# Branch, merge and output projections of a hybrid decoder step as three single-pass products, with the splitting on three engines

## The reference, cut to what matters

```python
def back(x, gates, y_ssm, y_swa, y_mem, lw):
    gt = jax.nn.sigmoid(gates.astype(jnp.float32)).astype(x.dtype)
    gt = gt.reshape(gates.shape[0], gates.shape[1], N_BRANCHES, D_MODEL)
    merged = (gt[:, :, 0] * jnp.einsum('ble,ed->bld', y_ssm, lw['w_br_ssm'])
              + gt[:, :, 1] * jnp.einsum('ble,ed->bld', y_swa, lw['w_br_swa'])
              + gt[:, :, 2] * jnp.einsum('ble,ed->bld', y_mem, lw['w_br_mem']))
    x1 = x + jnp.einsum('bld,de->ble', merged, lw['w_out'])
    b, L = x1.shape[0], x1.shape[1]
    h = rms_norm(x1, lw['norm2_g']).reshape(b * L, D_MODEL)
    return x1 + hier_moe(h, lw).reshape(b, L, D_MODEL)
```

## Time and profile before

| | us |
|---|---|
| median of 3 runs | 1034.17 (1033.91 to 1037.94) |
| the profiled execution | 1034.25 |
| its span, first to last instruction | 1032.4 |
| TensorE busy | 925.0 |
| VectorE, ScalarE, GpSimd busy | 460.8, 261.7, 189.3 |

### The profile page before, as it was taken

How to read it: one execution, slowest core, us unless ns; L and a number is a source line. 1 busy time by engine, 2 the same in 40 slices (tenths; PEclk the granted TensorE clock), 3 DMA queues, 4 the chain that set the end, 5 groups by cost and what they waited for, 6 DMA issues and landing times. The chain is left out here.

```text
span 1032.4 us, 14711 instructions
## 1 busy us (share of the span) xinstructions
PE 925.0 (90%) x6134; PEld 723.4 (70%) x6134; DVE 460.8 (45%) x800; ACT 261.7 (25%) x448; POOL 189.3 (18%) x91
## 2 busy tenths in 40 slices
PE   4899968899999896887879999999996999998888
PEld 3899968799988784554657677888785655554454
DVE  3621988932277636685376941111214122222222
ACT  5347433335344453322123230000001001010100
POOL 2347754326300003022212320000000000000000
PEclk9899988979999997898889999999995799998899
DMA  6354713323522213664556979547463479999992
GB/s 248 135 203 134 275 52 117 136 83 123 169 82 83 67 62 123 243 241 164 167 204 202 377 242 398 213 175 273 145 263 123 164 325 421 422 422 422 422 422 116
DMA packets 33640, 223.41 MB, mean 216 GB/s; under 512 B 3776, under 2 KB 4048, under 8 KB 9008
## 3 DMA queue, kind: packets, MB, share of 16 engines
q1 hardware_dynamic: 28048, 199.57, 49.8%
q0 software_dynamic: 5536, 23.06, 6.8%
HBM read 207.29 MB, written 15.31 MB: 216 GB/s over the span
## 5 line engine op out<-in xcount | busy, mean ns | idle before, releaser
L469 PE MATMUL bank<-at_r,at_r 128*128 128x264 f32 (+1 forms) x1152 | 153.9, 297 | 23.4 <-POOL at_r L229 16.2
L469 PEld LDWEIGHTS bank<-at_r,at_r 128*128 128x128 f32 x1152 | 150.3, 200 | 25.6 <-POOL at_r L229 18.0
L457 PE MATMUL bank<-HN,W 128*128 128x264 f32 x640 | 157.4, 401 | 0.0
L229 POOL TENSOR_TENSOR at_r<-W,at_r 128x1024 fp32r<-128x1024 f32 x52 | 128.3, 2473 | 124.3 <-ACT at_r L1264 124.2
L457 PEld LDWEIGHTS bank<-HN,W 128*128 128x128 f32 x640 | 124.5, 198 | 30.8 <-issue 9.6
L1237 ACT ACTIVATE M<-bank 128x264 f32<-128x264 f32 (+4 forms) x140 | 59.2, 429 | 256.1 <-PE bank L469 101.5
L457 PE MATMUL bank<-M,W 128*128 128x264 f32 x384 | 87.7, 388 | 4.0 <-DMA W<-in_w_stream 1.6
L926 PE MATMUL bank<-M,W 128*128 128x128 f32 (+1 forms) x432 | 83.1, 326 | 3.3 <-DVE M L1977 3.3
L457 PEld LDWEIGHTS bank<-M,W 128*128 128x128 f32 x384 | 72.2, 190 | 17.3 <-DMA W<-in_w_stream 2.5
L926 PEld LDWEIGHTS bank<-M,W 128*128 128x128 f32 (+1 forms) x432 | 63.5, 202 | 24.6 <-issue 6.7
L1264 ACT ACTIVATE at_r<-W 128x1024 fp32r<-128x1024 f32 x60 | 62.5, 1053 | 0.6 <-DMA W<-in_w_stream 0.5
(11 more groups left out here) (318 smaller groups left out, 1086.1 us busy)
## 6 DMA issues: line engine op xcount, KB each, us to landing
W<-in_w_stream SPq DMA_DIRECT2D x70, 1024.0 KB, 4.9
M<-in_w_exp_gate SPq DMA_DIRECT2D x32, 1024.0 KB, 22.7
M<-in_w_exp_up SPq DMA_DIRECT2D x32, 1024.0 KB, 23.7
M<-in_w_exp_down SPq DMA_DIRECT2D x32, 1024.0 KB, 15.7
M<-in_state_ssm POOLq DMA_DIRECT2D x8, 1024.0 KB, 7.6
M<-in_mem_kT SPq DMA_DIRECT2D x8, 1024.0 KB, 5.9
out_s_ssm<-M POOLq DMA_DIRECT2D x8, 1024.0 KB, 11.7
M<-in_mem_v SPq DMA_DIRECT2D x8, 1024.0 KB, 7.2
```

The lines of the kernel that those rows point to most:

```text
L229: return eng.tensor_tensor(low, x, high.bitcast(F32), ALU.subtract)
L457: mm = pe.matmul(bank[:, 0:n], w[:, k, P * c:P * (c + 1)], x[:, k, 0:n], start=(k == 0), stop=(k == KT - 1))
L469: mm = pe.matmul(bank[:, 0:n], w[:, k, :], x_[:, k, 0:n], start=(k + i == 0), stop=(k == KT - 1 and i == 2))
```

## The change

Branch, merge and output products become split tiles. Each chunk gives two halves, numbered h = 0 to 39: window branch 0 to 7, memory branch 8 to 15, state-space branch 16 to 31 (each chunk pair: first part of both tiles, second part of both), output 32 to 39. ScalarE copies the high part of half h into one of three places, after half h-3 has been used; GpSimd makes the low part of even halves, VectorE of odd ones, in the place of the raw weights. The operands are split too: the attended window and memory operands after gate tile 29 on ScalarE and, after the last state store, on GpSimd; their sample columns on ScalarE and VectorE; y in two halves on ScalarE, then GpSimd and VectorE; MERGED tile by tile on ScalarE and VectorE. The window tiles all come ahead of the memory tiles. The sigmoid of the gates is taken in pieces from gate tile 29 on. The loads of the first experts' pieces go to other places, and later.

```diff
-for _i in range(4):
-    STREAM += [(("swa", _i), "w_br_swa", CW * _i, 0), (("memb", _i), "w_br_mem", CW * _i, 0)]
+for _name, _w in (("swa", "w_br_swa"), ("memb", "w_br_mem")):
+    STREAM += [((_name, _i), _w, CW * _i, 0) for _i in range(4)]
...
+        BRANCH = [("swa", i) for i in range(4)] + [("memb", i) for i in range(4)]
+        BRANCH += [(f"ssm{part}", i) for i in range(4) for part in "ab"] + [("out", i) for i in range(4)]
+        HALVES = 2 * len(BRANCH)
+        SWA_AT, MEMB_AT, SSM_AT, OUT_AT = 0, 8, 16, 32
...
 # TensorE
-            wait_drained(pe, ("mo", 3))
-            wait_drained(pe, "s_back")
-            for i in range(4):
-                for kind, x in (("swa", Q), ("memb", MQ)):
-                    w = arrive((kind, i))
-                    for c in range(2):
-                        feature_tile((kind, 2 * i + c), w, c, x, T, (kind, i))
+            def branch_half(h, bank, x, first, start, stop):
+                pe.wait_ge(sem("branch_low1" if h % 2 else "branch_low0"), h // 2 + 1)
+                high, low = branch_high(h), branch_raw(h, w_low)
+                for k in range(KT):
+                    for i, (w, part) in enumerate(((high, 0), (high, 1), (low, 0))):
+                        mm = pe.matmul(bank[:, 0:T], w[:, k, :], x(part, first + k), start=(start and k + i == 0),
+                                       stop=(stop and k == KT - 1 and i == 2))
+                return mm
...
+            pe.wait_ge(sem("sample_split"), 1)
+            pe.wait_ge(sem("attended_low"), 1)
+            for m in range(8):
+                branch_tile(("swa", m), SWA_AT + m, swa_split)
+            pe.wait_ge(sem("attended_low"), 2)
+            for m in range(8):
+                branch_tile(("memb", m), MEMB_AT + m, memb_split)
...
-            pe.wait_ge(sem("merged"), 8)
+            pe.wait_ge(sem("merged_low"), 8)
...
 # SP
-                if name == ("memb", 0):
+                if name == ("swa", 2):
+                    sp.wait_ge(sem("s_v_out"), 16)
+                    load_piece("gate", 0, 0, 0)
+                    sp.dma_start(HN, ins["xT"]).then_inc(sem("x_again"), 16)
+                elif name == ("swa", 3):
                     wait_filled(sp, "s_back")
-                    wait_filled(sp, ("mo", 3))
-                    sp.wait_ge(sem("s_v_out"), 16)
                     sp.wait_ge(sem("samples_done"), 1)
...
+                elif name in (("memb", 0), ("memb", 1)):
+                    load_piece("gate", 2 + name[1], 0, 2 + name[1])
+                elif name == ("ssmb", 0):
+                    wait_filled(sp, ("memb", 7))
                     load_piece("up", 0, 0, 0)
+                elif name == ("ssma", 1):
                     load_piece("up", 1, 0, 1)
                 elif name == ("ssmb", 1):
                     load_piece("up", 2, 0, 2)
+                elif name == ("ssmb", 2):
+                    wait_filled(sp, "ss_y")
                     load_piece("up", 3, 0, 3)
...
             sp.wait_ge(sem("merged"), 8)
-            load_piece("down", 3, 0, 3)
+            for j in range(3):
+                load_piece("down", j, 0, j)
...
             wait_filled(sp, ("out", 7))
+            load_piece("down", 3, 0, 3)
...
 # GpSimd, after the last state store
+            pool.wait_ge(sem("attended_high"), 1)
+            low_part(nc.gpsimd, SWA_SPLIT[1][:, :, 0:SEQ], Q[:, :, 0:SEQ], SWA_SPLIT[0][:, :, 0:SEQ]
+                     ).then_inc(sem("attended_low"), 1)
+            pool.wait_ge(sem("attended_high"), 2)
+            for half in range(2):
+                four = slice(4 * half, 4 * half + 4)
+                last = low_part(nc.gpsimd, MEMB_LOW[:, four, 0:SEQ], MQ[:, four, 0:SEQ], MEMB_HIGH[half][:, :, 0:SEQ])
+            last.then_inc(sem("attended_low"), 1)
             pool.wait_ge(sem("ring_in0"), 160 + 16 * BATCH_S)
             pool.dma_start(outs["s_swa_v"], RING[0]).then_inc(sem("s_v_out"), 16)
             pool.wait_ge(sem("samples_done"), 1)
             pool.dma_start(WR, ins["w_router"].rearrange("(k p) n -> p k n", p=P)).then_inc(sem("router_in"), 16)
+            for h in range(0, HALVES, 2):
+                pool.wait_ge(sem("branch_high"), h + 1)
+                low_part(nc.gpsimd, branch_raw(h, w_low), branch_raw(h, apart["W"]), branch_high(h)
+                         ).then_inc(sem("branch_low0"), 1)
+                if h == 12:
+                    pool.wait_ge(sem("y_high"), 1)
+                    low_part(nc.gpsimd, Y_LOW[:, 0:8, :], C[:, 0:8, :], Y_HIGH[0]).then_inc(sem("y_low0"), 1)
...
 # ScalarE
+            def branch_highs(h):
+                if h >= 3:
+                    half_used(act, h - 3)
...
+                a.activation(branch_high(h), branch_raw(h, apart["W"]), ACT.Copy).then_inc(sem("branch_high"), 1)
...
+                if i == 40:
+                    act.wait_ge(sem("samples_done"), 1)
+                    wait_filled(act, "s_out")
+                    branch_highs(0)
+                    branch_highs(1)
...
+                if i == 29:
...
+                    a.activation(SWA_SPLIT[0][:, :, 0:SEQ], Q[:, :, 0:SEQ], ACT.Copy).then_inc(sem("attended_high"), 1)
...
+                    for half in range(2):
+                        last = a.activation(MEMB_HIGH[half][:, :, 0:SEQ], MQ[:, 4 * half:4 * half + 4, 0:SEQ], ACT.Copy)
+                    last.then_inc(sem("attended_high"), 1)
...
-            a.activation(at("G"), at("G"), ACT.Sigmoid).then_inc(sem("gates_active"), 1)
...
+                if h in (10, 12):
+                    half = (h - 10) // 2
+                    a.activation(Y_HIGH[half], C[:, 8 * half:8 * half + 8, :], ACT.Copy).then_inc(sem("y_high"), 1)
...
 # VectorE
+            for high, low, part in sample_parts(b):
+                last = low_part(v, low, part, high)
...
+            for m in range(8):
+                b = wait_filled(dve, ("memb", m))
+                drains(v.tensor_tensor(TQ, b[:, 0:T], G[:, 16 + m, :], ALU.mult), ("memb", m))
+                wait_drained(dve, ("memb", m))
+                link(v.tensor_tensor(MERGED[:, m, :], MERGED[:, m, :], TQ, ALU.add))
+                branch_lows(MEMB_AT + m + 3)
+                if m == 4:
+                    dve.wait_ge(sem("y_high"), 2)
+                    low_part(v, Y_LOW[:, 8:16, :], C[:, 8:16, :], Y_HIGH[1]).then_inc(sem("y_low1"), 1)
...
+                for m_ in (m - 1, m):
+                    b = wait_filled(dve, ("ssm", m_))
+                    drains(v.tensor_tensor(TQ, b[:, 0:T], RS, ALU.mult), ("ssm", m_))
+                    wait_drained(dve, ("ssm", m_))
+                    link(v.tensor_tensor(TQ, TQ, G[:, m_, :], ALU.mult))
+                    done(dve, v.tensor_tensor(MERGED[:, m_, :], MERGED[:, m_, :], TQ, ALU.add), "merged")
+                    branch_lows(SSM_AT + 4 * (m_ // 2) + 2 + m_ % 2 + 3)
+                    if m_:
+                        merged_lows(m_ - 1)
+            merged_lows(7)
```

More of the change, by code:

```diff
@@ new lines, in branch_raw, with half_used, sample_parts @@
+        def branch_raw(h, tensor):
+            o = CHUNK * (number[BRANCH[h // 2]] % WBUFS)
+            return tensor[:, o:o + CHUNK].rearrange("p (k n) -> p k n", n=CW)[:, :, P * (h % 2):P * (h % 2 + 1)]
+        def half_used(eng, h):
+            kind, i = BRANCH[h // 2]
+            if kind == "ssma":
+                eng.wait_ge(sem("ssma_used"), 2 * i + h % 2 + 1)
+            else:
+                wait_filled(eng, ("ssm" if kind == "ssmb" else kind, 2 * i + h % 2))
+        def sample_parts(b):
+            parts = []
+            for dt in range(2):
+                src = b[:, P * dt:P * (dt + 1)].rearrange("p (h c) -> p h c", h=MEM_H)[:, :, 0:BATCH_S]
+                for half in range(2):
+                    parts.append((MEMB_HIGH[half][:, dt::2, SEQ:T], MEMB_LOW[:, 4 * half + dt:4 * half + 4:2, SEQ:T],
+                                  src[:, 2 * half:2 * half + 2, :]))
+            for hh in range(2):
+                rows = slice(64 * hh, 64 * (hh + 1))
+                src = b[rows, 2 * P:3 * P].rearrange("p (g b j hh) -> p g j b hh", g=KV, j=2, hh=2)[..., hh]
+                high, low = (x[rows, :, SEQ:T].rearrange("p (g j) b -> p g j b", j=2) for x in SWA_SPLIT)
+                parts.append((high, low, src))
+            return parts
@@ L846, in _ @@
             pe.wait_ge(sem("y_squared"), 2)
             squares("ss_y", 3, Z, 0, XS_T, T)
-            pe.wait_ge(sem("y_ready"), 1)
             for i in range(4):
-                wa = arrive(("ssma", i))
                 banks = [next_proj(("ssm", 2 * i + c)) for c in range(2)]
                 for part in range(2):
-                    w = arrive(("ssmb", i)) if part else wa
+                    if i == 0:
+                        pe.wait_ge(sem(f"y_low{part}"), 1)
                     for c in range(2):
-                        for k in range(KT):
-                            mm = pe.matmul(banks[c][:, 0:T], w[:, k, P * c:P * (c + 1)], C[:, KT * part + k, :],
```

(14 more changed lines are left out.)

158 lines of the change are left out of this document (95 added, 63 removed).

## The result

The kernel after takes 1025.76 us (median of 8 runs, 1021.09 to 1031.54), the kernel before 1039.37 in 8 runs taken beside it: a ratio on record of 0.989, with an interval of 0.987 to 0.992. Run again later, the two gave 1027.22 and 1037.23, ratio 0.989 (0.987 to 0.992). The medians stand 13.6 and 10.0 us apart. So it is faster by 1.1%, some 11 us; forecast were 4.1 us. The predicted time, 1030.1, is 4.3 us above the median and the range held it. That it came so near is luck in part: it was counted down from 1034.25, a short run of the kernel before, and the saving itself was forecast at well under half. The profiled execution of after took 1025.45 us, its span is 1023.7.

A forecast was written before the change was run, and what follows sets the result against it. TensorE, busy 90% of the span, was taken to bound the kernel. Savings of 27.2 us less 12.9, 5.2 and 5.0 gave 4.1, from 1034.25 to 1030.1 us; range 1021 to 1040.

The forecast's parts named there:

- window and memory tiles: Window and memory branches: 16 single-pass tiles at 2.95 us replace 59.3 us, gain 12.1 us.
- state-space tiles: State-space branch: 16 half tiles go from 57.1 to 47.2 us, gain 9.9 us.
- output tiles: Output product: 8 tiles go from 3.62 to 2.95 us each, gain 5.2 us.
- start of the stage: First branch tile: operand splitting delays it from 613.10 to 623.7, 10.6 us, plus 2.3 for the clock; 12.9 us lost.
- tile 13: Sixth memory tile: VectorE's low part waits for GpSimd's, gap 3.5 us plus 1.7 for the clock; 5.2 us lost.
- ahead of the output product: After the last merge add: VectorE's low parts wait for GpSimd's, gap 4.7 instead of 1.53, clock 1.8; 5.0 us lost.
- the hard case: VectorE and GpSimd, two SBUF operands: VectorE waits for GpSimd's whole operation and the next one if already queued.
- the prediction's own sign: Profile after: first branch tile before 618, or both later gaps under 1.5 us, would show the two-engine step wrong.
- its step on the two engines: VectorE and GpSimd delay each other at three places, charged 12.9, 5.2 and 5.0 us.
- the first rival: VectorE gets its turn between two GpSimd operations: tile 13 4.05 us less, start 0.7 less, 1025.4 us; chance 0.22.
- The slower rival: Weight chunks land too late for splitting and stop TensorE; decides above 9.5 us of landing, 1050 at 11; chance 0.18.
- an unfavourable end of 2.4: Tile 6: its chunk, loaded behind the wait for the values' store, could be 2.4 us late; nothing charged.

The follow-up runs named there:

- experiment 5: Kernel after with the eight window tiles taken back to float32, nothing split for them: 1025.19 us, ratio 0.987 to the kernel before.
- experiment 8: Kernel after with float32 window tiles, GpSimd's output low part behind the merge's, last but one state store behind the small transfers: 1019.28 us, ratio 0.982.
- experiment 9: Kernel after with float32 window tiles, weights' and y's low parts on VectorE, merge's last ahead of weights', later state store: 1019.16 us, ratio 0.982.
- experiment 4: Kernel after with one wait added: GpSimd makes the output product's first low part only behind VectorE's last merge low parts: 1023.24 us, ratio 0.987.
- experiment 6: Kernel after run once more, no edit: 1027.22 us.
- Experiment 2: Kernel before with SP's waits for the stores moved behind the load of the second window chunk: 1040.43 us, ratio 1.002.
- experiment 7: Kernel after with all low parts of weights and y on VectorE, none on GpSimd: 1024.73 us, ratio 0.988.
- experiment 3: Kernel before with only the order changed, all window tiles ahead of the memory tiles: 1039.9 us, ratio 1.002.

## Why the prediction was right in most parts and short in its sum

| term, us | forecast | measured |
|---|---|---|
| window and memory tiles | 12.1 | 12.1 (59.3 less 50.36, plus the 1.02 and the 2.1 that are counted below) |
| state-space tiles | 9.9 | 10.1 |
| output tiles | 5.2 | 5.1 (54.06 to 51.49 up to the experts, plus 2.6 counted below) |
| start of the stage | -12.9 | -10.5 (idle 9.16 instead of 0.75, clock 2.1) |
| tile 13 | -5.2 | -1.0 |
| ahead of the output product | -5.0 | -5.4 (4.35 instead of 1.53, clock 2.6) |
| sum | 4.1 | 10.4 |

**Saving.** The price of a single-pass tile, taken from the earlier trace rows, held in all three products; the work of feeding them was hidden, in the state-space branch without a gap.

**Tile 13: the term that was mis-sized, and most of the error.** I took the hard case, in which VectorE waits for two GpSimd operations in a row. In the trace it waited for one (VectorE, then GpSimd, of after):

```profile
659.33 5.50 DVE L237 TENSOR_TENSOR at_r<-W,at_r 128x1024 fp32r<-128x1024 f32 x1 [0.20 <-ACT at_r L1440]
...
658.74 5.02 POOL L237 TENSOR_TENSOR at_r<-M,at_r 128x2112 fp32r<-128x2112 f32 x1
663.72 3.37 POOL L237 TENSOR_TENSOR at_r<-W,at_r 128x1024 fp32r<-128x1024 f32 x1
```

VectorE's 1.23 us operation came 0.6 us behind GpSimd's and ended 1.1 us after its end; GpSimd's next, 2.35 alone, took 3.37, so this time it was GpSimd that waited. The gap was 1.0 to 1.6 us in every profile in which GpSimd made these parts, with no loss of clock. By the prediction's own sign, a gap under 1.5 us, its step on the two engines is wrong here, and the first rival was right. The Trainium skill ("SBUF — State Buffer", "Who interferes with whom") gives the shared ports to whichever of the two issues first, for its whole instruction; the trace agrees at this tile, 5.50 us behind one operation of 5.02, and not everywhere, as the last section shows.

**Start.** The first tile came at 623.47, forecast 623.7. That it fits so well is luck: this execution was 1.85 us late already at the gate tiles, and against those the start is 8.5 us later, not 10.6. The chain of waits of after runs here through GpSimd's queue: the last state store, the three low parts of the operands, two issues, the low part of the first weights.

```profile
608.50 1.15 POOL out_s_ssm L1270
...
609.67 9.85 POOL at_r L237 x3
...
620.97 2.36 POOL at_r L237
```

From the end of the three low parts to the tile it took 3.95 us, not 5.2. VectorE's sums, which I had kept waiting for all three, got a turn behind each (2.2 to 2.3 us each; priced for the rival at 0.7 only) and held nothing up. The other 0.8 us is that the low parts ended sooner, counted from the gate tiles. Experiments 5, 8 and 9 show that the term is the splitting itself: without the window's share of it the idle time is 0.90 in all three. In experiment 5 the late transfer could have hidden the rest; in 8 and 9 TensorE's wait for that was only 2.4 us.

**Output.** Forecast 4.7 us of gap and 1.8 of clock, measured 4.35 and 2.6; experiment 4 shows the cause of the gap, as argued. The clock's part varies, 1.5 and 1.3 behind the same gap in experiments 6 and 5.

**Chunks.** The slower rival did not come about: no tile of after waits for a chunk. Experiment 2 has 2.50 us at the tile for which I kept an unfavourable end of 2.4, but with four transfers ahead of that chunk; after has two. In after the store landed in 4.86 us, not 13.46, and the chunk, issued at 631.91 when its buffer came free, landed at 636.54. In experiments 8 and 9, too, no tile waited for it.

So of the 6.3 us between forecast and measurement 4.2 are tile 13 and 2.4 the start, with 0.4 the other way ahead of the output product. The first rival's time, 1025.4, was the nearest, at tile 13 for its reason; that it lies within 0.4 us of the median is luck, since its saving, 8.9 us, is 1.6 short of the traces'.

## What to carry to other kernels

Where splitting feeds TensorE, the steady state is cheap; look at the first tile of a stage, where the operand's own splitting stands open. Leaving that first product unsplit can be the better bargain: its eight tiles took 28.39 us instead of eight times 2.95, 4.8 more, and took away 8.3 us of idling and its colder clock. What is left of that depends on the waits ahead: from the last pairs of gate tiles to the end of both branches it is 77.5 us in before, 77.1 in after, 74.1 in experiment 7 and 72.2 in experiment 9, but 80.3 in experiment 5, where the late transfer stood open. An operation that the next stage waits for should neither stand behind another in its own queue (1.0 us in experiment 7) nor beside one of GpSimd's (1.9 us in experiment 4). And a wait that is taken away uncovers the next one: price the transfers that it had hidden.

## What the runs showed of the hardware that was not expected

**Turns between VectorE and GpSimd.** In after VectorE was served between two GpSimd operations at tile 13 and three times at the start, but not at 621.08, where an operation on 128 columns lasted through both of two queued ones:

```profile
612.77 2.19 DVE L1969 TENSOR_TENSOR M<-M 128x128 f32<-128x128 f32 x1
...
621.08 4.72 DVE L1980 TENSOR_TENSOR M<-M 128x128 f32<-128x128 f32 x1
...
609.67 9.85 POOL L237 TENSOR_TENSOR at_r<-M,at_r 128x2048 fp32r<-128x2048 f32 x3
...
620.97 4.67 POOL L237 TENSOR_TENSOR at_r<-W,at_r 128x1024 fp32r<-128x1024 f32 x2
```

That is the same kind of row as the 6.76 and 5.12 us of the earlier trace rows. In the row of 5.12 us VectorE's operation began 0.3 us ahead of GpSimd's first, by the records (195.70 and 196.00), and yet lasted through both; the prediction reads it as behind them. What decides who goes next was not found; a forecast has to carry both cases.

**A small transfer behind a store.** A 1 KB transfer that lands in 1.7 us took 6.12 and 5.71 in the two profiles in which it was issued within 1.3 us behind a 1 MB store of another queue. Why the load ahead of it took 8.0 to 8.9 us in some profiles and 10.1 to 10.6 in four is open; the kernel after shows both.

**The clock behind a gap.** Gaps of 2.44 and 2.41 us ahead of the output product were followed by three tiles in 10.58 us (experiment 4) and in 9.01 (experiment 9). The same gap of 4.35 us was followed by 11.58, 10.55 and 10.35 us (after, experiments 6 and 5), and one of 2.18 us by a loss of 1.3 (experiment 3). So the length of the gap alone does not say what the clock takes; what does is open.
